# Top-k threshold search: candidates from ScalarE and two small VectorE operations a bit; index projections dealt out between score heads

## The reference, cut to what matters

```python
q, c, qi, ki, wi = split(h @ w_in)            # 16 query heads, latent 256, 8 index heads of 64, index key, weights
qi = rope(qi) * 64 ** -0.5;  ki = rope(ki);  wi = wi * 8 ** -0.5
rel = relu(einsum('bqhd,bsd->bqhs', qi, ki))  # 8 heads
score = einsum('bqh,bqhs->bqs', wi, rel)
score = where(key <= query, score, NEG_INF)
_, sel = lax.top_k(score, 256)                # then attention over the chosen keys, softmax over those <= query
```

## Time and profile before

| | us |
|---|---|
| runs (3): lowest, median, highest | 3314.23, 3317.99, 3318.42 |
| profiled execution | 3313.27 |
| its span, first to last instruction | 3311.4 |
| mean granted TensorE clock | 0.94 of full |

### The profile page before, as it was taken

One profiled execution on the slowest core, in us unless ns is written; L12 is line 12 of the kernel. 1 busy time (PEld: TensorE's weight loads), 2 busy tenths in 40 slices (PEclk: granted clock), 3 DMA queues, 4 the chain that ended last, 5 costly groups with the idle time before them and its releaser, 6 DMA issues.

```text
span 3311.4 us, 35561 instructions
## 1 busy us (share of the span) xinstructions
PE 2954.5 (89%) x12424; PEld 2233.1 (67%) x12424; DVE 2072.8 (63%) x3708; ACT 1511.4 (46%) x2593; POOL 277.7 (8%) x221
## 2 busy tenths in 40 slices
PE   7797999999879999999968685479997999999997
PEld 5685556665667888878856564245566788887885
DVE  6544455554267776677675699754426777667656
ACT  4343555555344544444433554445434454444443
POOL 2352000000000000000003034130000000000000
PEclk9887999999989999999989798689998999999999
DMA  5133121111323333333313012442142233333332
GB/s 169 44 99 108 46 53 40 52 47 40 125 66 94 96 96 96 96 96 93 98 58 111 1 53 81 102 141 52 33 126 66 89 96 98 93 96 96 105 102 73
DMA packets 356617, 275.05 MB, mean 83 GB/s; under 512 B 58085, under 2 KB 308007, under 8 KB 355927
## 3 DMA queue, kind: packets, MB, share of 16 engines
q1 hardware_dynamic: 355287, 270.68, 27.6%
q10 hardware_dynamic: 1152, 2.10, 0.2%
HBM read 238.18 MB, written 31.92 MB: 82 GB/s over the span
## 4 chain that ended last, share of the span: by engine, by line
PE 76%; DVE 12%; ACT 4%; issue 3%; DMA 3%; SPq 1%; POOL 0%; POOLq 0%; DVEq 0%; ACTq 0%
PE PS L491 18%; PE PS L492 18%; PE PS L493 18%; PE PS L909 10%; PE PS L830 3%; PE PS L884 3%; PE PS L885 3%; DVE m_MASK L2290 2%; PE PS L890 1%; DVE m_Z L2364 1%; DVE m_PRED L2295 1%; DVE RT_b L596 1%; DMA WR<-in_nsa_w_out 1%; PE PS L645 1%; PE PS L902 1%
## 5 line engine op out<-in xcount | busy, mean ns | idle before, releaser
L491 PE MATMUL PS<-HH,WH 128*128 128x512 f32 (+1 forms) x2160 | 857.4, 397 | 91.8 <-POOL WL L464 47.6
L492 PE MATMUL PS<-HL,WH 128*128 128x512 f32 (+1 forms) x2160 | 849.3, 393 | 0.0
L493 PE MATMUL PS<-HH,WL 128*128 128x512 f32 (+1 forms) x2160 | 847.9, 393 | 0.0
L491 PEld LDWEIGHTS PS<-HH,WH 128*128 128x128 f32 x2160 | 414.3, 192 | 186.4 <-issue 56.5
L492 PEld LDWEIGHTS PS<-HL,WH 128*128 128x128 f32 x2160 | 413.7, 192 | 86.6 <-issue 2.5
L493 PEld LDWEIGHTS PS<-HH,WL 128*128 128x128 f32 x2160 | 413.2, 191 | 86.2
L480 DVE TENSOR_TENSOR WL<-WR,WH 128x1024 fp32r<-128x1024 f32 x290 | 354.2, 1221 | 111.4 <-ACT WH L473 99.4
L473 ACT ACTIVATE WH<-WR 128x1024 fp32r<-128x1024 f32 x290 | 308.1, 1062 | 123.8 <-PE PS L493 90.2
L929 ACT ACTIVATE n_PX<-PS 128x512 f32<-128x512 f32 (+1 forms) x320 | 173.0, 544 | 223.3 <-PE PS L890 114.2
L1028 DVE CUSTOM_DVE_ANT_0 n_JUNK<-PS,n_MZ 128x512 bf16<-128x512 f32 (+2 forms) x320 | 147.9, 488 | 116.8 <-PE PS L830 116.5
L460 POOL TENSOR_TENSOR TOUCH<-WR 128x1 f32<-128x1 f32 x45 | 10.1, 225 | 1867.5 <-PE PS L493 1029.5
(11 more groups left out here) (375 smaller groups left out, 5166.9 us busy)
## 6 DMA issues: line engine op xcount, KB each, us to landing
WR<-in_ffn_w_up SPq DMA_DIRECT2D x176, 512.0 KB, 3.7
WR<-in_ffn_w_down SPq DMA_DIRECT2D x88, 512.0 KB, 3.4
WH<-qh_save SPq DMA_DIRECT2D x64, 256.0 KB
n_RB<-r_save SPq DMA_DIRECT2D x96, 128.0 KB, 2.9
WR<-in_nsa_w_out SPq DMA_DIRECT2D x16, 512.0 KB, 3.8
WL<-ql_save SPq DMA_DIRECT2D x32, 256.0 KB
WR<-in_dsa_w_in SPq DMA_DIRECT2D x16, 512.0 KB, 4.0
WR<-in_dsa_w_out SPq DMA_DIRECT2D x16, 512.0 KB, 4.0
```

Source lines behind the costliest of these rows:

```text
L491: nc.tensor.matmul(dst, wh, xh, start=start, stop=False)
L492: nc.tensor.matmul(dst, wh, xl, start=False, stop=False)
L493: return nc.tensor.matmul(dst, wl, xh, start=False, stop=stop)
```

## The change

In the search, ScalarE makes CM = CAND + LESS (an Identity activation with a per-partition bias column of -half a step) ahead of its signs; VectorE waits for its last count, compares, and makes PRED x step + CM in one scalar_tensor_tensor. The table PW of powers gives way to LESS with 16 columns. In the scores, `queries` takes a range of k-steps with the two banks' products side by side in each step. Queries 1 runs 4 k-steps before scores 0 and one after each of its first 4 heads; queries 2 and 3 run one k-step after each of the first 8 heads of scores 1 and 2. The turns and ropes that follow move: round 1's to n = 5 of round 0 (parts at 8), round 2's turn to n = 8 of round 1 on ScalarE too, round 3's to n = 8 of round 2 (parts at 10).

```diff
-            queries(0)
-            queries(1)
-            scores(0, 0, 12)
+            queries(0, 0, DT)
+            queries(1, 0, 4)
+            for n in range(12):
+                scores(0, n, n + 1)
+                if n < 4:
+                    queries(1, 4 + n, 5 + n)
...
-            scores(1, 0, 6)
-            queries(2)
-            scores(1, 6, 12)
+            for n in range(12):
+                scores(1, n, n + 1)
+                if n < 8:
+                    queries(2, n, n + 1)
...
-            queries(3)
-            scores(2, 0, 12)
+            for n in range(12):
+                scores(2, n, n + 1)
+                if n < 8:
+                    queries(3, n, n + 1)
...
 # queries(j, k0, k1): waits only if k0 == 0, then
+                for k in range(k0, k1):
+                    for dst, tok in ((PS[:, 6, T - IQ:HALF], slice(T - IQ, HALF)),
+                                     (bank(7), slice(HALF, T))):
                         last = product(dst, wh[:, k, :], wl[:, k, :], HH[:, k, tok], HL[:, k, tok],
                                        k == 0, k == DT - 1)
...
 # ScalarE
-            index_turn(1, 3)
             for n in range(12):
                 relu(0, n)
-                if n == 1:
+                if n == 5:
+                    index_turn(1, 3)
+                if n == 8:
                     index_high(1, 3)
...
-                if n == 7:
+                if n == 8:
                     index_turn(2, 6)
...
-            index_turn(3, 7)
             for n in range(12):
                 relu(2, n)
-                if n == 1:
+                if n == 8:
+                    index_turn(3, 7)
+                if n == 10:
                     index_high(3, 7)
...
                 act.wait_ge(S["cand"], bit + 1)
+                x = 14 - bit if bit < 15 else 30 - bit
+                nc.scalar.activation(M["CM"][:, :], M["CAND"][:, :], ACT.Identity,
+                                     bias=M["LESS"][:, x:x + 1])
...
 # VectorE, a bit of the search
-                    nc.vector.tensor_scalar(tile_of("MASK", i), tile_of(source, i), CAND[:, i - 2:i - 1],
-                                            None, ALU.is_lt, ALU.add, accum_out=CNT[:, i - 2:i - 1])
-                link1(dve, nc.vector.tensor_tensor(M["CM"][:, :], CAND[:, :],
-                                                   PW[:, x:x + 1].broadcast_to([P, 6]), ALU.subtract))
+                    last = nc.vector.tensor_scalar(tile_of("MASK", i), tile_of(source, i),
+                                                   CAND[:, i - 2:i - 1], None, ALU.is_lt, ALU.add,
+                                                   accum_out=CNT[:, i - 2:i - 1])
+                link1(dve, last)
                 dve.wait_ge(S["sgn"], before + bit + 1)
                 link1(dve, nc.vector.tensor_tensor(M["PRED"][:, :], CNT[:, :], KT[:, :], ALU.is_le))
-                link1(dve, nc.vector.tensor_tensor(M["STEP"][:, :], M["PRED"][:, :],
-                                                   PW[:, x + 1:x + 2].broadcast_to([P, 6]), ALU.mult))
...
-                step = nc.vector.tensor_tensor(dst[:, :], M["CM"][:, :], M["STEP"][:, :], ALU.add)
+                step = nc.vector.scalar_tensor_tensor(out=dst[:, :], in0=M["PRED"][:, :],
+                                                      scalar=float(1 << x), in1=M["CM"][:, :],
+                                                      op0=ALU.mult, op1=ALU.add)
...
 # VectorE, scores: index_rope(1, 3) from ahead of the second reciprocal to n == 5 of round 0,
 # index_low(1, 3) from n == 1 to 8; index_rope(3, 7) from n == 0 to 8 of round 2, index_low(3, 7) from 2 to 10
```

More of the change, by code:

```diff
@@ L346, in trunk @@
                 ("R", [P, 2, T], F32), ("THR", [P, 2, 6], I32), ("TA", [P, 6], F32),
-                ("TB", [P, 6], F32), ("CAND", [P, 6], F32), ("CM", [P, 6], F32), ("STEP", [P, 6], F32),
+                ("TB", [P, 6], F32), ("CAND", [P, 6], F32), ("CM", [P, 6], F32),
                 ("CNT", [P, 6], F32), ("PRED", [P, 6], F32), ("KK", [P, 6], F32),
@@ L351, in trunk @@
                 ("NEED", [P, 6], F32), ("KCON", [P, 6], F32), ("KMUL", [P, 6], F32),
-                ("PW", [P, 17], F32)):
+                ("LESS", [P, 16], F32)):
             M[name] = sb("m_" + name, shape, dt, scope)
@@ L2039, in sums, with queries @@
                     last.then_inc(S["sum"], 1)
-            def queries(j):
+            def queries(j, k0, k1):
                 info = L1["i"][j]
                 wh, wl = weights(info)
[L2044 to L2051, removed]
+                if k0 == 0:
+                    pe.wait_ge(w_split, info["n"] + 1)
+                    if j == 0:
+                        pe.wait_ge(S["root"], 2)
+                    else:
+                        pe.wait_ge(S["rot"], (3, 4, 7)[j - 1])
+                        pe.wait_ge(S["t1"], (3, 4, 7)[j - 1])
+                for k in range(k0, k1):
+                    for dst, tok in ((PS[:, 6, T - IQ:HALF], slice(T - IQ, HALF)),
+                                     (bank(7), slice(HALF, T))):
                         last = product(dst, wh[:, k, :], wl[:, k, :], HH[:, k, tok], HL[:, k, tok],
                                        k == 0, k == DT - 1)
-                last.then_inc(i_mm, 1)
+                if k1 == DT:
+                    last.then_inc(i_mm, 1)
             def scores(j, n0, n1):
@@ L2280, in threshold_bits @@
         def threshold_bits(dve, source, bits, before):
-            S, CNT, CAND, KT, PW = sem1, M["CNT"], M["CAND"], M["KT"], M["PW"]
+            S, CNT, CAND, KT = sem1, M["CNT"], M["CAND"], M["KT"]
             link1(dve, nc.vector.tensor_tensor(KT[:, :], M["KK"][:, :], M["TMUL"][:, :], ALU.mult))
@@ L2376, in prep1_dve @@
             nc.vector.memset(M["KDB"][0:1, :, :].bitcast(F32), -1.0)
-            for e in range(17):
-                nc.vector.memset(M["PW"][:, e:e + 1], 2.0 ** (e - 1))
+            for e in range(16):
+                nc.vector.memset(M["LESS"][:, e:e + 1], -(2.0 ** (e - 1)))
             for i in range(2, QT):
@@ L2406, in prep1_dve @@
             index_low(0, 2)
-            index_rope(1, 3)
             link1(dve, nc.vector.reciprocal(M["E1"][:, HALF:T], M["E1"][:, HALF:T]))
@@ L2418, in prep1_dve @@
                 accumulate(0, n)
-                if n == 1:
+                if n == 5:
+                    index_rope(1, 3)
+                if n == 8:
                     index_low(1, 3)
@@ L2441, in prep1_dve @@
                 accumulate(2, n)
-                if n == 0:
+                if n == 8:
                     index_rope(3, 7)
-                if n == 2:
+                if n == 10:
                     index_low(3, 7)
```

## The result

The changed kernel takes 3296.3 us (median of 4 runs, 3294.07 to 3299.48), the kernel before 3318.2 beside it (4 runs): a ratio of 0.9937 [0.992, 0.9955], 21.9 us less. The forecast was 3285, 31 less than the base, in a range of 3271 to 3305. By the profiled executions it is 3294.07 us (span 3292.3) against 3313.27 (3311.4): 19.2. Measured again, the changed kernel took 3287.9 against 3313.85: 0.9919 [0.9906, 0.9931].

The account below looks back on a forecast made before the run. Hand-overs bound the scores; VectorE's bits, partly waiting for GpSimd, bound the search. Search -26 and scores -5 make -31 us: 3282 from the profile, 3287 from the median, so 3285 predicted, range 3271 to 3305.

Parts of the forecast that it names:

- A bit and ScalarE's operation: Top-k search: an undisturbed bit falls from 3.73 to 3.46 us; ScalarE's added 0.2 us stays hidden.
- GpSimd's ring: Search: GpSimd's work, ScalarE's copy, SP and DMA set 13.5 us a pair instead of 15.97; both halves together -26.
- VectorE's waits: Search: VectorE operations reading two SBUF tiles wait for GpSimd; some 2 us a pair, fitting inside the ring.
- Rival (a): Search: VectorE's stalls behind GpSimd stay, a pair takes 14.7 us, total 3299; chance 0.22.
- The scores: Indexer's scores: dealing out projections removes 20.2 us of VectorE waits and adds 15.3, so -5.
- three ropes behind turns: Scores: ScalarE's turn shows some 2.6 of its 3.24 us in each of three rounds, 7.8 together.
- the heads of round 2: Scores: TensorE gives a head every 1.6 us against VectorE's 0.95, for eight heads: 5.2 us of waits.
- (b): Scores lose with TensorE at the lower clock, +8 instead of -5; 3298 with part 1 at -18; chance 0.10.
- (c): Search: ScalarE reloads activation tables every bit, 3328; chance 0.05, including ScalarE late in another way.
- What follows (masks, attention) starts that much earlier and is the same: Behind the search: masks and attention keep their length, so the whole -31 us reaches the end.

Follow-up runs that it names:

- the three runs that took away the one, the other and both: Changed kernel with a second projection buffer, 3293.38 us; with KT and CM in PSUM, 3290.85; with both and ScalarE's high part one bit later, 3275.22.
- the delayed run: Changed kernel with VectorE clearing a 1024-column buffer four times between the last threshold and the masks: 3292.05 us, 0.9938.
- added products: Changed kernel with 74 unread products on idle TensorE, 3287.23 us; with 12 more and GpSimd's first late query behind tile 4's mask, 3287.46.

## Why the prediction was right, and which step failed

- **A bit and ScalarE's operation.** Predicted 3.46 us and 0.2 net, hidden. Undisturbed bits took 3.46 (2058.44 to 2061.90, the starts of their first counts), the operation 0.299, 0.1 more than taken from the nearest row, and still hidden in these; over all 31 bits VectorE waited for ScalarE's signs 5.2 us, in five waits. By the figure of the Trainium skill ("ScalarE: Activation LUTs", What ACT_TABLE_LOAD costs) the estimate was 0.285; the trace agrees.
- **GpSimd's ring.** Predicted 13.5 a pair, 63.8 and 61.1 us; measured 13.3 to 13.6 (12.3 for the last, predicted 12.4), 63.7 and 61.0. That the ring holds and that VectorE's waits are next fits the three runs that took away the one, the other and both: a loss in the search, nothing, and the gain. The third also took away ScalarE's wait at the high part, which the prediction had priced only in the second half, so it does not show that two limits are all there were.
- **Rival (a)**, the stalls stay, was near: with 0.07 us more a bit (3.53) and GpSimd's start earlier by ScalarE's operation, two pairs of the first half stalled before the ring caught them.
- **The scores.** Predicted -5, measured -5.1 at the last accumulation. The terms were less exact: three ropes behind turns waited 2.35, 2.22 and 2.23 us (6.8 for 7.8), the heads of round 2 waited 8.6 in eight idles (for 5.2).
- **Rivals (b) and (c)** did not happen: the scores gained at a mean clock of 0.82 (0.81 before), and no table load was added. (In (c), 2.5 + 2.57 is 5.07 and not 5.05; nothing hangs on it.)
- **The step that failed** is "What follows (masks, attention) starts that much earlier and is the same". It starts 31.5 us earlier and is not the same: 6.9 us are given back in the stretch, which the clock's low time accounts for (28.4 - 14.3 = 14.1, half of it 7.0), and 5.5 more behind it in the first execution, which the second did not repeat; for that part no cause beyond the clock's later dips was tested. The granted clock does not rise at a set time after the attention's first product: it rose 20.6 us into the stretch in both executions of the changed kernel, 12.7 in the delayed run, and 10.5 to 13.0 in the other nine without added products. The Trainium skill ("TensorE: Matmul & The Clock Gate", What's actually happening) says that the chip's watch on TensorE runs freely and does not start anew with a kernel; the delayed run agrees in so far as the same work, 4.3 us later, met the rise after 12.7 us instead of 20.6. The prediction had read the mean clock of the scores and none of the stage behind the search, where TensorE had idled for 53 us ahead of the attention.
- **Luck in the number.** By the medians 21.9 us were won, and 26.0 in the second measurement, against 31 in the sum. The result lies in the range because that reached to -11 for rivals (a) and (b), and neither of them is what took the difference.

## What to carry to other kernels

Where two limits lie just behind each other (here a ring of engines and VectorE's waits for GpSimd), an experiment that removes one can show nothing or a loss; remove both before calling either free. A gain ahead of a stage that starts with TensorE at its low clock need not be passed on one to one: compare the stage's length and granted clock, and look at more than one execution before explaining the last microseconds.

## What the runs showed of the hardware

A VectorE operation of 6 columns with one operand in SBUF and one in PSUM was never held up by GpSimd: 160 to 163 ns in 62 operations, where two SBUF operands took up to 1258 ns in the same places. The Trainium skill ("SBUF — State Buffer", Who interferes with whom) says that a VectorE instruction with at most one SBUF input, outside VectorE's two-port modes, does not contend with GpSimd; the 160 to 163 ns agree.
